# Conditioning weights stationary in TensorE in plain fp32, spread over three stages; layer 1's rows kept in SBUF; column block outermost in the dense matmuls

## The chip, the cores and the metric
The kernel runs on one core of a Trainium2 chip. The time is the device time of one execution in microseconds, as a median of several executions.

## The reference, cut to what matters
Two post-norm transformer layers over 1056 rows (1024 of a prompt, 32 of a sample) of width 1024, in fp32. Each layer first computes six conditioning vectors per sequence from a conditioning vector c, one c for the prompt and one for the sample:

```
mod = (silu(c) @ w_ada + b_ada)[:, None, :]        # w_ada: 1024 x 6144
sh1, sc1, g1, sh2, sc2, g2 = split(mod, 6)
u = layer_norm(x) * (1 + sc1) + sh1
... = split(u @ w_in)                              # queries, keys, values, gates
oa, ob, oc, state = mix_fn(...)                    # three groups of attention heads
o = concatenate([group_rms(oa), group_rms(ob), group_rms(oc)]) * g_out
x = layer_norm(ALPHA * x + g1 * (o @ w_out)) * ln1_g + ln1_b
u = layer_norm(x) * (1 + sc2) + sh2
f = square(relu(u @ w1)) @ w2                      # 1024 -> 4096 -> 1024
x = layer_norm(ALPHA * x + g2 * f) * ln2_g + ln2_b
```

The two columns of `silu(c)` are all that the conditioning multiplies: a matrix of 1024 x 6144 by two vectors. sh1 and sc1 are wanted first, g1 after the attention, sh2 and sc2 before the MLP, g2 in it. Outputs are the rows y and the attention caches.

## The kernel before, in words
A prologue and, per layer, a sequence of stages. Each stage is a block: all engines start it together and the next one starts when every queue is through. Inside a block each engine has its own queue in program order, and semaphores order the engines. SP issues all DMAs from its queue, in order.

- Prologue (L231 on): masks, silu(c) in `c_silu`, bias rows. SP copies the input rows into the output tensor `x_states`, and the block waits for that copy.
- Conditioning stage (L508 on): rows are loaded from `x_states` into `x_all` (nine tiles of 128 rows, the last of 32), VectorE takes mean and variance (`tile_stats`, `tile_figures`), POOL normalises the tiles in place (L539). The 24 chunks of w_ada (1 MB each, 128 x 2048, six buffers) are split by ScalarE and VectorE into two fp32r parts (L589, L617). TensorE holds `c_parts` as weights and streams the chunk in 16 pairs of 256 columns (L555): the result is a row of 256 values on 4 partitions, copied by ScalarE to `ada_v`. Once all chunks are through, small plain fp32 matmuls (L563: weights 4 x 128, 2 moving columns) turn the rows into columns: 16 of the 48 vectors' tiles before the first row tile is turned, then four after each further one. Then each row tile is turned by TensorE (`turn`, L445), scaled and shifted by ScalarE and VectorE (`scale_shift`, `scale_shift_rest`) and split into `u_hi` and `u_lo` (`split_turned`). POOL splits the first two weight chunks of the projection in the meantime (`pool_split`, L343, L345).
- Projection stage, attention stages: `three_pass` (L358) multiplies an fp32 weight chunk, split in two fp32r parts, with the split rows: three products of 128x128 weights with 352 columns, for each of three column blocks, each block in a PSUM bank of its own. The head outputs go to DRAM (`scr_o`).
- Output-projection stage (L1365 on): rows are loaded from `scr_o`, RMS-normalised (ScalarE L1411, VectorE L1448, POOL L1380), turned (L1391, L445), scaled by ScalarE (L1419), split by VectorE (L416, L418), and only when all nine tiles are through the projection begins (L1398).
- Post-norm stage (L1478 on): the projected columns are turned back (L1510) while SP loads the x tiles into two buffers (`x_tile`, L1485). VectorE adds and takes statistics (L1555). Two weight chunks for the MLP are loaded between x tile 3 and x tile 4 (L1493). Then the rows are normalised (ScalarE L1533), get gain (VectorE L1565) and bias (POOL L1501), are turned (L1517), copied to `acc` (ScalarE L1539, which takes its turn between the normalisations), normalised again (L1577), turned (L1522), modulated and split.
- MLP stage: 4608 matmuls of `three_pass`. Final stage (L1688 on): turned back, normalised, stored to `x_states[l + 1]`. After it POOL clears the layer's 148 semaphores one by one (L1756).

Of the kernel before, what the change touches and what calls it, by code (L numbers as in the profile page):

```python
# [17 lines left out]
F32 = mybir.dt.float32  # L18
# [42 lines left out]
def rows_of(t):  # L61
    return P if t < NPT else DEC

def build(nc, io):
    scr_o = nc.dram_tensor("scr_o", [T, D], F32, kind="Internal").ap()
    scr_a = nc.dram_tensor("scr_bias_a", [AH, P * EXT_A], F32, kind="Internal").ap()
# [16 lines left out]
    with ExitStack() as ctx:  # L84
# [17 lines left out]
        join = keep("join", [4, 2])  # L102
# [24 lines left out]
        ADA_SLOTS = 6  # L127
        ada_w = [at(f"w_ada{s}", U0 + s * 8192, [P, CW]) for s in range(ADA_SLOTS)]
        x_all = at("row_tiles", Q0 + 42240, [P, NTT, D])
        c_pad = at("c_zeros", U0 + ADA_SLOTS * 8192, [P, P])  # L130
        c_st = at("c_parts", U0 + ADA_SLOTS * 8192 + 512, [P, KT, P], F32R)
        ada_v = at("ada_rows", Q0 + 8192, [4, 256 * (ADA_CH + 2)])
# [96 lines left out]
        pro_ext, pro_edges, pro_x = sem("pro_ext_loaded"), sem("pro_ext_edges"), sem("pro_x_copied")  # L229
        with nc.Block() as block:  # L230
            @block.sync  # L231
            def _(sp):
# [8 lines left out]
                sp.dma_start(io["x_states"][0, 0:SEQ, :], io["x_prompt"][0]).then_inc(pro_x, 16)  # L241
                sp.dma_start(io["x_states"][0, SEQ:T, :], io["x_sample"][0]).then_inc(pro_x, 16)
# [6 lines left out]
                sp.wait_ge(pro_x, 64)  # L249
                sp.wait_ge(pro_bias, 16 * (1 + DEPTH))  # L250
# [23 lines left out]
            def _(dve):  # L274
# [16 lines left out]
                dve.tensor_tensor(join[:], ident[0:4, 0:2], ident[0:4, 2:4], ALU.add).then_inc(pro_act, 1)  # L291

# [4 lines left out]
        ada_in = [S(f"ada_loaded{s}") for s in range(ADA_SLOTS)]  # L297
        ada_hi, ada_lo, ada_used, par_in, mod_step, ada_sum, ada_clear, ada_turned, ada_c = S("ada_high"), S("ada_low"), S("ada_used"), S("params_loaded"), S("mod_steps"), S("ada_summed"), S("ada_margin"), S("ada_turned"), S("ada_c_parts")
# [59 lines left out]
        def three_pass(pe, out, s, cols, a_hi, a_lo):  # L358

            n = len(cols)
            for k, c in enumerate(cols):
                for w, a in ((w_hi, a_hi), (w_hi, a_lo), (w_lo, a_hi)):
                    for b in range(3):
                        mm = pe.matmul(out[:, b, :], w[s][:, c:c + P], a[:, k, b * NB:(b + 1) * NB],  # L365
                                       start=(k == 0 and w is w_hi and a is a_hi),
                                       stop=(k == n - 1 and w is w_lo))
            return mm
# [81 lines left out]
        row_in = [S(f"rows_loaded{t}") for t in range(NTT)]  # L450
# [55 lines left out]
        for l in range(DEPTH):  # L506

            with nc.Block() as block:  # L508
                @block.sync
                def _(sp):  # L510
                    for t in range(NTT):
                        r = rows_of(t)
                        sp.dma_start(x_all[0:r, t, :], io["x_states"][l, t * P:t * P + r, :]).then_inc(row_in[t], 16)
# [4 lines left out]
                    with sp.Fori(0, ADA_CH // ADA_SLOTS) as j:  # L518
                        for s in range(ADA_SLOTS):
                            sp.wait_ge(ada_lo, ADA_SLOTS * j + (s + 1))  # L520
                            sp.dma_start(ada_w[s][:], io["w_all"][l * CHUNKS + ADA_SLOTS * j + s]).then_inc(ada_in[s], 16)

# [3 lines left out]
                def _(pool):  # L526

                    own = Own(pool, ada_c)
                    own.did(pool.memset(c_pad[:], 0.0))
                    own.settle()  # L530
                    own.did(pool.tensor_copy(c_st[:, :, 4:P], c_pad[:, 4:P].rearrange("p (a b) -> p a b", a=1)
                                             .broadcast_to([P, KT, P - 4])))
                    own.did(pool.tensor_copy(c_st[:, :, 0:2], c_silu[:]))
                    own.settle()
                    own.did(pool.tensor_tensor(c_st[:, :, 2:4], c_silu[:], c_st[:, :, 0:2].bitcast(F32), ALU.subtract))
# [6 lines left out]
                    split_stream_free(pool)  # L542
                    pool.wait_ge(ada_used, ADA_CH + 2)
                    pool_weights(pool, 0, 2)

                @block.tensor
                def _(pe):
                    pe.sem_inc(ada_used, 2)
                    pe.wait_ge(ada_c, 4)
                    with pe.Fori(0, ADA_CH // ADA_SLOTS) as j:  # L550
                        for s in range(ADA_SLOTS):
                            pe.wait_ge(ada_lo, ADA_SLOTS * j + (s + 1 + ADA_SLOTS))
                            for k in range(KT):
                                for w in (w_hi, w_lo):
                                    mm = pe.matmul(psum[:, 4 + s % 2, 0:256], c_st[:, k, :],  # L555
                                                   w[s % 2][:, k * 256:(k + 1) * 256],
                                                   start=(k == 0 and w is w_hi), stop=(k == KT - 1 and w is w_lo))
                            mm.then_inc(ada_used, 1)

                    def turn_vectors(first, last):  # L560
                        for m in range(first, last):
                            c0 = 512 + m * P
                            mm = pe.matmul(psum[:, 6 + (first > 0), 2 * m:2 * m + 2], ada_v[:, c0:c0 + P], join[:],  # L563
                                           start=True, stop=True)
                        return mm
                    pe.wait_ge(ada_sum, ADA_CH + 2)
                    turn_vectors(0, 16).then_inc(ada_turned, 1)
# [7 lines left out]
                    mm.then_inc(ada_turned, 1)  # L575

                @block.scalar
                def _(act):
                    load_tables(act)
                    tile_roots(act, NTT, 1, r_var, r_log, r_root)  # L580
                    act.wait_ge(ada_clear, 1)
                    with act.Fori(0, ADA_CH // ADA_SLOTS) as j:
                        for s in range(ADA_SLOTS):
                            act.wait_ge(ada_in[s], 16 * j + 16)
                            act.wait_ge(ada_used, ADA_SLOTS * j + (s + 1))

                            act.activation(ada_v[:, bass.ds(256 * ADA_SLOTS * j + 256 * s, 256)],
                                           psum[0:4, 4 + s % 2, 0:256], ACT.Copy).then_inc(ada_sum, 1)
                            act.activation(w_hi[s % 2][:, 0:CW], ada_w[s][:], ACT.Copy).then_inc(ada_hi, 1)  # L589
                    for s in (ADA_SLOTS - 2, ADA_SLOTS - 1):  # L590
                        act.wait_ge(ada_used, ADA_CH + 2 - (ADA_SLOTS - 1 - s))
                        c0 = 256 * (ADA_CH + s - ADA_SLOTS + 2)
                        act.activation(ada_v[:, c0:c0 + 256], psum[0:4, 4 + s % 2, 0:256], ACT.Copy)\
                            .then_inc(ada_sum, 1)
                    for t in range(NTT):
                        if t == 0:
                            act.wait_ge(mod_step, 3)
# [4 lines left out]
                def _(dve):  # L602
                    own = Own(dve, a_dve)

                    dve.memset(psum[0:4, 4:6, 0:256], 0.0).then_inc(ada_clear, 1)
                    dve.sem_inc(ada_lo, ADA_SLOTS)
                    figures_begin(own)
                    for t in range(NTT):
                        dve.wait_ge(row_in[t], 16)
# [4 lines left out]
                    with dve.Fori(0, ADA_CH // ADA_SLOTS) as j:  # L614
                        for s in range(ADA_SLOTS):
                            dve.wait_ge(ada_hi, ADA_SLOTS * j + (s + 1))
                            dve.tensor_tensor(w_lo[s % 2][:, 0:CW], ada_w[s][:], w_hi[s % 2][:, 0:CW].bitcast(F32),  # L617
                                              ALU.subtract).then_inc(ada_lo, 1)

                    def vectors(n, first, last, scales):  # L620

                        dve.wait_ge(ada_turned, n + 1)
                        sums = psum[:, 6 + n, 0:96].rearrange("p (m c) -> p m c", c=2)
                        for c in range(2):
                            dve.tensor_tensor(mods[:, first:last, c], sums[:, first:last, c], b_ada[:, first:last],
                                              ALU.add).then_inc(mod_step, 1)
                        dve.wait_ge(mod_step, 3 * n + 2)
# [850 lines left out]
            with nc.Block() as block:  # L1478
                @block.sync
                def _(sp):  # L1480
# [366 lines left out]
```

## Time and profile before
| | us |
|---|---|
| median of 3 runs (3662.45 to 3667.59) | 3666.75 |
| the profiled execution, its own time | 3663.84 |
| span of its instructions | 3662.0 |

### The profile page before, as it was taken

The page shows a single profiled execution, that of the slowest core. Times are in us where ns is not written, and L with a number is a line of the kernel's source. Part 1 is how long each engine was busy: PE and PEld are TensorE (multiplying, and loading weights), DVE is VectorE, ACT ScalarE, POOL GpSimd, SP SyncE. Part 2 cuts the span into 40 slices and gives each one's busy share as a digit, 9 for nine tenths or more (in the row PEclk, how much of TensorE's full clock was granted, in tenths as well). Part 3 has the DMA queues.
Part 4 walks back from the last instruction along what each step waited for, and adds up shares of the span by engine and source line. Part 5 has one row for each costly group of instructions (what it writes and reads, how often), then busy time and mean ns, then how long its engine had stood idle before and what let it go on. Part 6 is the DMA issues. An engine that isn't in the chain of part 4 may idle for free. (4 is left out here: it accounts for less than half of the span.)

```text
span 3662.0 us, 50730 instructions
## 1 busy us (share of the span) xinstructions
PE 3098.5 (85%) x19938; PEld 2958.0 (81%) x19938; DVE 1521.5 (42%) x3371; ACT 917.2 (25%) x1906; POOL 1202.8 (33%) x567
## 2 busy tenths in 40 slices
PE   3799889669589999999537998896594899999994
PEld 3799879449489999999537997894493899999993
DVE  5501278450643333333655013884507333333335
ACT  3411266341320000000234113663413100000002
POOL 2122355111324444333221223651113333344441
PEclk9799999679689999999877998996795899999997
DMA  7322023320211111110173121233202111111101
GB/s 303 121 72 89 16 71 73 120 84 0 82 47 46 46 45 40 42 45 35 58 280 127 43 75 26 66 77 114 81 0 82 47 46 46 46 46 46 46 23 59
DMA packets 112569, 257.09 MB, mean 70 GB/s; under 512 B 42402, under 2 KB 78790, under 8 KB 94352
## 3 DMA queue, kind: packets, MB, share of 16 engines
q1 hardware_dynamic: 112416, 255.05, 20.5%
q8 instruction: 96, 1.57, 0.2%
q14 instruction: 57, 0.47, 0.0%
HBM read 216.40 MB, written 38.12 MB: 70 GB/s over the span
## 5 line engine op out<-in xcount | busy, mean ns | idle before, releaser
L343 POOL CAST w_hi<-w_raw 128x2048 fp32r<-128x2048 f32 (+1 forms) x92 | 174.4, 1896 | 1324.6 <-DVEq L1679 362.1
L365 PE MATMUL psum<-u_hi,w_hi 128*128 128x352 f32 x2592 | 565.5, 327 | 19.6 <-ACT L209 9.2
L365 PE MATMUL psum<-u_lo,w_hi 128*128 128x352 f32 x2592 | 562.7, 326 | 0.0
L365 PE MATMUL psum<-u_hi,w_lo 128*128 128x352 f32 x2592 | 561.6, 325 | 0.0
L1682 DVE SCALAR_TENSOR_TENSOR acc_t<-psum,mods,acc_t 128x704 f32<-128x704 f32 (+2 forms) x768 | 401.0, 578 | 298.6 <-PE psum L365 298.6
L365 PEld LDWEIGHTS psum<-u_hi,w_hi 128*128 128x128 f32 x2592 | 445.8, 190 | 20.8 <-issue 20.7
L345 POOL TENSOR_TENSOR w_lo<-w_raw,w_hi 128x2048 fp32r<-128x2048 f32 (+1 forms) x92 | 450.5, 4897 | 7.4
L365 PEld LDWEIGHTS psum<-u_lo,w_hi 128*128 128x128 f32 x2592 | 447.2, 190 | 0.0
L365 PEld LDWEIGHTS psum<-u_hi,w_lo 128*128 128x128 f32 x2592 | 443.5, 190 | 0.0
L1669 DVE TENSOR_TENSOR h_relu<-h_relu 128x1056 f32<-128x1056 f32 x64 | 103.1, 1612 | 696.6 <-ACT h_relu L1659 696.6
L1659 ACT ACTIVATE h_relu<-psum 128x1056 f32<-128x1056 f32 x64 | 67.5, 1054 | 1161.8 <-PE psum L365 1161.8
L365 PE MATMUL psum<-h_hi,w_hi 128*128 128x352 f32 x1536 | 332.3, 324 | 0.0
L365 PE MATMUL psum<-h_lo,w_hi 128*128 128x352 f32 x1536 | 329.8, 323 | 0.0
L365 PE MATMUL psum<-h_hi,w_lo 128*128 128x352 f32 x1536 | 329.0, 323 | 0.0
L1612 POOL TENSOR_TENSOR h_lo<-h_relu,h_hi 128x1056 fp32r<-128x1056 f32 x64 | 158.2, 2472 | 379.6 <-ACT h_hi L1661 370.0
L445 PE MATMUL psum<-ident,row_tiles 128*128 128x128 f32 (+1 forms) x576 | 130.3, 406 | 159.5 <-POOL row_tiles L1501 48.3
L365 PEld LDWEIGHTS psum<-h_hi,w_hi 128*128 128x128 f32 x1536 | 263.3, 188 | 0.0
L365 PEld LDWEIGHTS psum<-h_lo,w_hi 128*128 128x128 f32 x1536 | 260.8, 188 | 0.0
L365 PEld LDWEIGHTS psum<-h_hi,w_lo 128*128 128x128 f32 x1536 | 259.7, 188 | 0.0
L445 PEld LDWEIGHTS psum<-ident,row_tiles 128*128 128x128 f32 (+1 forms) x576 | 106.9, 220 | 178.5 <-POOL row_tiles L1501 55.5
L555 PE MATMUL psum<-w_hi,c_parts 128*128 128x256 f32 x384 | 108.0, 315 | 165.6 <-DVE w_lo L617 165.0
L555 PEld LDWEIGHTS psum<-w_hi,c_parts 128*128 128x128 f32 x384 | 81.0, 211 | 175.2 <-DVE w_lo L617 175.2
(198 smaller groups left out, 5091.5 us busy)
## 6 DMA issues: line engine op xcount, KB each, us to landing
w_raw<-in_w_all SPq DMA_DIRECT2D x86, 1024.0 KB, 4.8
w_ada<-in_w_all SPq DMA_DIRECT2D x48, 1024.0 KB, 5.6
row_tiles<-out_x_states SPq DMA_DIRECT2D x16, 512.0 KB, 7.2
scr_o<-o_head SPq DMA_DIRECT2D x32, 256.0 KB, 2.7
row_tiles<-scr_o SPq DMA_DIRECT2D x16, 512.0 KB, 7.1
x_tile<-out_x_states SPq DMA_DIRECT2D x16, 512.0 KB, 4.3
out_x_states<-row_tiles SPq DMA_DIRECT2D x16, 512.0 KB, 2.7
w_raw<-in_w_v SPq DMA_DIRECT2D x6, 1032.0 KB, 4.8
```

The costliest lines, as they stand in the source:

```text
L343: pool.tensor_copy(w_hi[s][:, 0:c], raw[s][:, 0:c]).then_inc(pool_step, 1)
L345: pool.tensor_tensor(w_lo[s][:, 0:c], raw[s][:, 0:c], w_hi[s][:, 0:c].bitcast(F32), ALU.subtract).then_inc(pool_step, 1)
L365: mm = pe.matmul(out[:, b, :], w[s][:, c:c + P], a[:, k, b * NB:(b + 1) * NB], start=(k == 0 and w is w_hi and a is a_hi), stop=(k == n - ...
L445: mm = pe.transpose(dst[:, k, 0:r], src[0:r, k * P:(k + 1) * P], ident[0:r, 0:r])
L555: mm = pe.matmul(psum[:, 4 + s % 2, 0:256], c_st[:, k, :], w[s % 2][:, k * 256:(k + 1) * 256], start=(k == 0 and w is w_hi), stop=(k == KT ...
L1612: pool.tensor_tensor(h_lo[par][:, m, :], h_r[m][:], h_hi[par][:, m, :].bitcast(F32), ALU.subtract).then_inc(h_rdy, 1)
L1659: act.activation(h_r[m][:].rearrange("p (b c) -> p b c", c=NB), lin[m], ACT.Relu).then_inc(h_ev[m], 1)
L1669: dve.tensor_tensor(h_r[m][:], h_r[m][:], h_r[m][:], ALU.mult).then_inc(h_sqd, 1)
L1682: ins = dve.scalar_tensor_tensor(a, lin[m % 2][:, b0:b1, c0:c1], mods[:, 40 + m, c:c + 1], a, ALU.mult, ALU.add)
```

## The change
The chunks of w_ada are no longer split. Each of their 128x128 blocks stands in TensorE as weights, in plain fp32, and the two columns of `c_silu` are the moving operand, so that the result comes out as columns in one PSUM bank and nothing has to be turned. Of the 24 chunks eight stay in the conditioning stage, eight go between the turns of the output-projection stage, eight between the two groups of turns of the post-norm stage; `add_bias` adds b_ada where each eight are through. The rows of layer 0 and its first eight chunks are loaded in the prologue; in layer 1 the rows are those that the final stage left in `x_all`, and its first eight chunks are loaded during that stage. `x_states` is gone: x tiles are read from the inputs or from a DRAM tensor between the layers. `three_pass` now goes through the column blocks outermost and takes (w_hi, a_hi), (w_lo, a_hi), (w_hi, a_lo) in each. The post-norm stage uses two PSUM tiles in turn instead of four.

```diff
+        def conditions(pe, chunk, w):
+            for m in (2 * chunk, 2 * chunk + 1):
+                for k in range(KT):
+                    c0 = 256 * k + P * (m % 2)
+                    mm = pe.matmul(psum[:, 6, 2 * m:2 * m + 2], w[:, c0:c0 + P], c_silu[:, k, :],
+                                   start=(k == 0), stop=(k == KT - 1))
+            return mm
+        def add_bias(dve, first, last, scales, done):
+            sums = psum[:, 6, 0:96].rearrange("p (m c) -> p m c", c=2)
+            for c in range(2):
+                dve.tensor_tensor(mods[:, first:last, c], sums[:, first:last, c], b_ada[:, first:last],
+                                  ALU.add).then_inc(mod_step, 1)
...
@@ three_pass
-            for k, c in enumerate(cols):
-                for w, a in ((w_hi, a_hi), (w_hi, a_lo), (w_lo, a_hi)):
-                    for b in range(3):
+            for b in range(3):
+                for k, c in enumerate(cols):
+                    for w, a in ((w_hi, a_hi), (w_lo, a_hi), (w_hi, a_lo)):
...
@@ prologue, SP
-                sp.dma_start(io["x_states"][0, 0:SEQ, :], io["x_prompt"][0]).then_inc(pro_x, 16)
-                sp.dma_start(io["x_states"][0, SEQ:T, :], io["x_sample"][0]).then_inc(pro_x, 16)
+                for t in range(NTT):
+                    sp.dma_start(x_all[0:rows_of(t), t, :], x_rows(0, t)).then_inc(row_x[t], 16)
+                    if t < 8:
+                        sp.dma_start(ada_w[t][:], io["w_all"][t]).then_inc(ada_in[t], 16)
...
@@ conditioning stage, TensorE (the splits on ScalarE and VectorE, and turn_vectors, are gone)
+                    for s in range(8):
+                        pe.wait_ge(ada_in[s], 32 * l + 16)
+                        conditions(pe, s, ada_w[s]).then_inc(ada_mm, 1)
                     for t in range(NTT):
                         pe.wait_ge(a_xn, t + 1)
...
                         turn(pe, tr2[t % 2], x_all[:, t, :], rows_of(t), a_turned)
-                        if 1 <= t <= 8:
-                            mm = turn_vectors(12 + 4 * t, 16 + 4 * t)
...
@@ output-projection stage, SP and TensorE
+                    for n, c in enumerate(ADA_F):
+                        if n >= 4:
+                            sp.wait_ge(ada_mm, 8 + n - 3)
+                        sp.dma_start(ada_f[n % 4][:], io["w_all"][l * CHUNKS + c]).then_inc(ada_fin[n % 4], 16)
                     sp_weights(sp, l, IN_CH + 2, OUT_CH - 2)
...
                         turn(pe, tr2[t % 2], x_all[:, t, :], rows_of(t), f_turned)
+                        if t >= 1:
+                            pe.wait_ge(ada_fin[(t - 1) % 4], 16 * ((t - 1) // 4 + 1))
+                            conditions(pe, ADA_F[t - 1], ada_f[(t - 1) % 4]).then_inc(ada_mm, 1)
...
@@ post-norm stage, SP and TensorE
                     for t in range(2, NTT):
                         x_tile(t)
                         if t == 3:
+                            for s, c in enumerate(ADA_G):
+                                sp.dma_start(ada_w[s][:], io["w_all"][l * CHUNKS + c]).then_inc(ada_in[s], 16)
                             sp_weights(sp, l, UP0, 2)
...
                         mm.then_inc(g_back, 1)
+                    for s, c in enumerate(ADA_G):
+                        pe.wait_ge(ada_in[s], 32 * l + 32)
+                        conditions(pe, c, ada_w[s]).then_inc(ada_mm, 1)
                     for t in range(NTT):
                         pe.wait_ge(g_x1, t + 1)
...
@@ final stage, SP
+                    if l + 1 < DEPTH:
+                        for s in range(8):
+                            sp.dma_start(ada_w[s][:], io["w_all"][(l + 1) * CHUNKS + s]).then_inc(ada_in[s], 16)
```

## Rows read from the trace of the kernel before
**Rows 1.** The page, parts 1 and 2: span, TensorE's busy time, its clock.
```profile
span 3662.0 us, 50730 instructions
...
PE 3098.5 (85%) x19938; PEld 2958.0 (81%) x19938; DVE 1521.5 (42%) x3371; ACT 917.2 (25%) x1906; POOL 1202.8 (33%) x567
...
PEclk9799999679689999999877998996795899999997
```
**Rows 2.** Busy time by stretch: from:to, length, engines, clock, DMA share, GB/s.
```profile
19.73:172.70 152.97, 92.82 (x552) 86.20 (x552) 97.97 (x101) 73.67 (x108) 33.34 (x17) 0.84 0.53 207
782.30:831.50 49.20, 15.80 (x72) 12.90 (x72) 34.10 (x79) 26.07 (x93) 13.52 (x9) 0.53 0.35 131
928.90:1034.50 105.60, 47.27 (x216) 37.89 (x217) 83.66 (x130) 41.46 (x78) 34.82 (x13) 0.56 0.20 72
1034.50:1781.30 746.80, 744.83 (x4608) 744.54 (x4608) 250.93 (x416) 68.53 (x64) 287.72 (x92) 1.00 0.12 42
1843.70:1993.90 150.20, 88.16 (x552) 81.39 (x552) 100.76 (x101) 73.60 (x107) 35.63 (x17) 0.77 0.55 211
```
**Rows 3.** Timeline of TensorE, layer 1's conditioning: start, duration, line, count, idle before.
```profile
1952.51 3.73 PE L563 MATMUL psum<-join,ada_rows 4*128 4x2 f32 x32 [0.46 <-ACT ada_rows L593]
1956.16 3.59 PE L445 MATMUL psum<-ident,row_tiles 128*128 128x128 f32 x16
1959.68 1.05 PE L563 MATMUL psum<-join,ada_rows 4*128 4x2 f32 x8
```
**Rows 4.** L563 by stretch: PE busy (x), PEld busy (x), clock, DMA share, GB/s.
```profile
1952.50:1956.10 3.60, 3.60 (x32) 3.60 (x32) 1.00 0.00 0
1956.20:1959.60 3.40, 0.03 (x1) 0.00 (x0) 0.51 0.00 0
147.90:149.80 1.90, 1.86 (x8) 1.78 (x8) 0.50 0.00 0
```
**Rows 5.** SP's issues from 0 to 180 us; GB/s in 40 slices of 20:60.
```profile
19.74 4.97 SPq L513 DMA_DIRECT2D row_tiles<-out_x_states  x9
...
GB/s 61 324 414 311 266 340 369 401 418 422 426 418 173 16 174 426 410 418 442 442 401 426 451 426 401 418 442 418 410 410 451 426 410 418 336 410 393 344 393 328
```
**Rows 6.** Timeline of POOL and VectorE, layer 0's conditioning stage.
```profile
39.89 19.78 POOL L539 TENSOR_SCALAR row_tiles<-row_tiles,tile_rsqrt 128x1024 f32<-128x1024 f32 x9 [18.44 <-DVE tile_rsqrt L408]
130.78 1.89 POOL L343 CAST w_hi<-w_raw 128x2048 fp32r<-128x2048 f32 x1 [71.11 <-PE psum L555]
132.76 4.51 POOL L345 TENSOR_TENSOR w_lo<-w_raw,w_hi 128x2048 fp32r<-128x2048 f32 x1
...
140.16 4.50 DVE L416 CAST u_hi<-turned_tile 128x1024 fp32r<-128x1024 f32 x1 [0.67 <-ACT turned_tile L428]
```
**Rows 7.** Timeline of TensorE, the front of layer 0's output projection.
```profile
801.98 3.68 PE L445 MATMUL psum<-ident,row_tiles 128*128 128x128 f32 x16 [22.44 <-POOL row_tiles L1380]
815.07 1.97 PE L445 MATMUL psum<-ident,row_tiles 128*128 128x128 f32 x8 [1.37 <-DVE u_lo L418]
821.35 1.97 PE L445 MATMUL psum<-ident,row_tiles 128*128 128x128 f32 x8 [1.37 <-DVE u_lo L418]
```
**Rows 8.** Timeline of POOL between the layers.
```profile
1843.76 0.20 POOL L529 MEMSET c_zeros<- 128x128 f32 x1 [13.76 <-POOLq L1757]
```
**Rows 9.** Layer 0's post-norm stage: timeline of TensorE, and a wait of VectorE.
```profile
949.16 1.97 PE L1510 MATMUL psum<-ident,attn_t 128*128 128x128 f32 x8 [2.84 <-DVE row_tiles L1555]
968.96 1.97 PE L445 MATMUL psum<-ident,row_tiles 128*128 128x128 f32 x8 [12.59 <-POOL row_tiles L1501]
...
DVE row_tiles L1555 <- DMA x_tile<-out_x_states: 7.9, 3, 3.1
```
**Rows 10.** Pitch: seven steps of the old conditioning (timeline); the value projection by stretch.
```profile
1948.74 0.28 PE L555 MATMUL psum<-w_hi,c_parts 128*128 128x256 f32 x1
1949.56 0.28 PE L555 MATMUL psum<-w_lo,c_parts 128*128 128x256 f32 x1
...
245.00:328.00 83.00, 81.58 (x648) 77.47 (x648) 1.00 0.21 76
```

More of the change, by code:

```diff
@@ L66, in build, with x_rows @@
     scr_o = nc.dram_tensor("scr_o", [T, D], F32, kind="Internal").ap()
+    x_mid = nc.dram_tensor("x_between_layers", [T, D], F32, kind="Internal").ap()
+    def x_rows(l, t):
+        if l == 0:
+            return io["x_prompt"][0, t * P:(t + 1) * P, :] if t < NPT else io["x_sample"][0]
+        return (x_mid if l == 1 else io["y_rows"])[t * P:t * P + rows_of(t), :]
     scr_a = nc.dram_tensor("scr_bias_a", [AH, P * EXT_A], F32, kind="Internal").ap()
@@ L228, in build @@
             sem("pro_loaded"), sem("pro_steps"), sem("pro_exp"), sem("pro_matmul"), sem("pro_bias_stored"))
-        pro_ext, pro_edges, pro_x = sem("pro_ext_loaded"), sem("pro_ext_edges"), sem("pro_x_copied")
+        pro_ext, pro_edges, pro_x = sem("pro_ext_loaded"), sem("pro_ext_edges"), sem("pro_selectors_loaded")
+        row_x = [sem(f"x_rows_loaded{t}") for t in range(NTT)]
+        ada_in = [sem(f"ada_loaded{s}") for s in range(8)]
         with nc.Block() as block:
@@ L296, in build @@
         pool_turn = S("pool_chunks_begun")
-        ada_in = [S(f"ada_loaded{s}") for s in range(ADA_SLOTS)]
-        ada_hi, ada_lo, ada_used, par_in, mod_step, ada_sum, ada_clear, ada_turned, ada_c = S("ada_high"), S("ada_low"), S("ada_used"), S("params_loaded"), S("mod_steps"), S("ada_summed"), S("ada_margin"), S("ada_turned"), S("ada_c_parts")
+        ada_fin = [S(f"ada_f_loaded{s}") for s in range(4)]
+        par_in, mod_step, ada_mm = S("params_loaded"), S("mod_steps"), S("ada_done")
+        def conditions(pe, chunk, w):
[10 more added lines that the diff above has]
+                                  ALU.add).then_inc(mod_step, 1)
+            if scales is not None:
+                dve.wait_ge(mod_step, done - 1)
+                dve.tensor_scalar(mods[:, scales:scales + 8, :], mods[:, scales:scales + 8, :], 1.0, None, ALU.add)\
+                    .then_inc(mod_step, 1)
         def split_stream_free(eng):
@@ L517, in _ @@
                     sp.dma_start(b_f[:], io["b_f"][bass.ds(l, 1), :].broadcast_to([P, CH])).then_inc(par_in, 16)
[L518 to L521, printed above, removed]
+                    if l == 0:
+                        sp.wait_ge(pro_bias, 16 * (1 + DEPTH))
+                        sp.wait_ge(pro_x, 32)
                     sp_weights(sp, l, 0, 2)
@@ L526, in _ @@
                 def _(pool):
[L528 to L535, printed above, removed]
+                    split_stream_free(pool)
                     pool.wait_ge(a_shift, 1)
@@ L547, in _ @@
                 def _(pe):
[L548 to L567, printed above, removed]
+                    for s in range(8):
+                        pe.wait_ge(ada_in[s], 32 * l + 16)
+                        conditions(pe, s, ada_w[s]).then_inc(ada_mm, 1)
                     for t in range(NTT):
@@ L580, in _ @@
                     tile_roots(act, NTT, 1, r_var, r_log, r_root)
[L581 to L594, printed above, removed]
+                    act.wait_ge(mod_step, 3)
                     for t in range(NTT):
-                        if t == 0:
-                            act.wait_ge(mod_step, 3)
                         act.wait_ge(a_turned, t + 1)
@@ L613, in _ @@
                     tile_figures(own, LN_EPS, 1, r_var, r_root, a_shift)
[L614 to L627, printed above, removed]
-                        dve.tensor_scalar(mods[:, scales:scales + 8, :], mods[:, scales:scales + 8, :], 1.0, None, ALU.add)\
-                            .then_inc(mod_step, 1)
                     dve.wait_ge(par_in, 64)
-                    vectors(0, 0, 16, 8)
+                    dve.wait_ge(ada_mm, 8)
+                    add_bias(dve, 0, 16, 8, 3)
                     for t in range(NTT):
@@ L634, in _ @@
                         split_turned(own, t, a_hi, a_lo)
-                    vectors(1, 16, 48, 32)
             K_EV = K_TILES
@@ L1516, in _ @@
                             pe.wait_ge(g_acc, t - 1)
-                        turn(pe, tr2[1 + t % 2], x_all[:, t, :], rows_of(t), g_x1t)
+                        turn(pe, tr2[t % 2], x_all[:, t, :], rows_of(t), g_x1t)
+                    pe.wait_ge(g_acc, NTT)
                     for t in range(NTT):
@@ L1521, in _ @@
                             pe.wait_ge(g_lo, t - 1)
[L1522 removed]
+                        turn(pe, tr2[t % 2], x_all[:, t, :], rows_of(t), g_xnt)
                 @block.scalar
@@ L1554, in _ @@
                         dve.wait_ge(g_back, t + 1)
-                        own.did(dve.scalar_tensor_tensor(y, x_sl[s][0:r, :], ALPHA, wide[3 * s][0:r, :],
+                        own.did(dve.scalar_tensor_tensor(y, x_sl[s][0:r, :], ALPHA, wide[s][0:r, :],
                                                          ALU.mult, ALU.add), g_y)
```

54 lines of the change are left out of this document (22 added, 32 removed).

## Prediction
> **What bounds the kernel now.** I read the page first, then the span cut at the stage borders, then the timelines of the stages that the diff touches. TensorE is busy 85% of the span [rows 1], and the cut says where not [rows 2]. The MLP (1034.5 to 1781.3) is TensorE at full clock without a gap: nothing there can be won but the pitch of its matmuls. The stages that the change edits are the other kind. The conditioning stage takes 153 us in layer 0 and 150 us in layer 1, the output-projection front (rows normalised and turned) 49 us with TensorE busy 15.8, the post-norm stage 105.6 us with TensorE busy 47.3, at a mean granted clock of 0.53 and 0.56. They are chains through four engines in which TensorE's queue waits. So each part is priced as a delay of such a chain.
>
> **What one chunk of conditioning costs after the change.** `conditions` issues 2 x 8 plain fp32 matmuls per chunk, 128x128 weights against 2 moving columns. The nearest operation of the trace is the turning of the vectors at L563: 128-column fp32 weights, 2 moving columns, plain fp32. It leaves two records per matmul (96 matmuls, 192 records). At full clock 32 records take 3.60 us (0.112 each); at half clock 8 take 1.86 us, which is seven steps of 0.213 and the last one's own length [rows 3, 4]. A chunk is 16 matmuls, 32 records: 3.6 us at full clock, 32 x 0.213 = 6.8 us at half. Eight chunks are 28.7 or 54.6 us; a layer has three such eights, 164 us of TensorE at half clock against 24 x 3.43 us = 82 now.
>
> **Which clock.** This decides the sign, and the trace has one passage on it. In layer 1 TensorE ran 1952.51 to 1956.24 nothing but L563 records, back to back, at granted clock 0.99; in the stretch right behind them the mean is 0.51, though transposes follow without a gap [rows 3, 4]. After the same number of transposes on end, 1956.16 to 1959.75, the next eight L563 records take 1.05 us, full clock again. In the interleaved part (a turn, eight L563 records, a turn) it stays at half [rows 3]. So a stream of two-column matmuls did not hold the full clock. I take half clock, 6.8 us per chunk. Against it: L563's weights fill 4 partitions, the new ones 128, and no row shows a long stream of those with few moving columns.
> The Trainium skill (TensorE: Matmul & The Clock Gate, "Why this matters for your kernels") says to keep TensorE continuously busy to get to the full clock. By that rule the conditioning streams run at 2.4 GHz and the change comes out faster; the L563 rows speak against it. It is the first rival below.
>
> **Layer 0, conditioning stage.** Now: a block switch at 19.7 behind the copy of the input rows, 24 chunks until 131, turns from 135.85, dense work from 172.88. After: the copy is gone and the prologue's SP issues 17 loads instead, 17 x 0.55 us (nine take 4.97 [rows 5]) from 3.64, then its three small stores: the stage starts at about 14.5. The loads are 12.6 MB; the queues moved about 0.42 MB per us [rows 5], so they land until about 36. VectorE's statistics end with the last row tile, thus POOL's normalising starts at about 39.2 against 39.89 now, and ends at 59; its two weight splits (12.9 us [rows 6]) end at 72. TensorE starts chunk 0 at 14.5 and is never short of data: 14.5 + 54.6 = 69. Then the turns. What follows was 37 us (135.85 to 172.88). The L563 records between the turns go; next late is the chain of turn, ScalarE, VectorE's cast and subtraction, two tiles deep: the output-projection front has exactly it, 6.28 us per two tiles (815.07 to 821.35) [rows 7]. First split at 74 (VectorE's cast took 4.50 us beside POOL's split [rows 6], which ends at 72), 7 x 3.15 more, last tile and block switch 2.5: dense work at 99. **Saved: 74.**
> **Layer 1.** The rows stay in SBUF and the eight chunks are loaded during the layer before, so TensorE starts at once: 1842.5 + 54.6 = 1897; statistics 14.7 (nine tiles of 1.63), POOL's 21.5 and 12.9 end at 1893 beside it. Then 6.4 for the first tile, 22 for seven, 2.5: dense work at 1928 against 1994.1. **Saved: 66**, of which 1.2 because 17 fewer of the 148 semaphores are cleared between the layers (POOL stands idle 13.76 us there, at most 0.09 us each [rows 8]). The same clearing at the end of the program: **1.2.**
>
> **Output-projection front, both layers.** Chunk t-1 stands in TensorE's queue behind turn t. Behind it wait the next turn, ScalarE, VectorE's split and then the projection. Now TensorE works from 801.98 to the border at 831.5, at the chain's pace [rows 2, 7]. After: eight turns of 1.71, the short one 0.9, eight chunks of 6.8: 69.2 us, TensorE bound, dense work at 871.5. The chunks' loads (behind the row loads on the queue) land by 799 to 807; a chunk reloaded after release has 30 us. The two weight loads now behind them on SP have 50 us. ScalarE's wait for the vectors is long met at its first read. **Lost: 40 per layer** (9 at full clock: 9 x 4.6 from 801.98).
>
> **Post-norm stage, both layers.** Two things add up. First the queue: SP issues eight 1 MB chunks between x tile 3 and x tile 4. Already two 1 MB weight loads there make tile 4 late: turn 5's successor starts after a 2.84 us wait for VectorE, which waited for x tiles 7.9 us in three times [rows 9]. Eight more MB at 0.42 MB per us are 19 to 20 us in front of tile 4; VectorE's row sums wait, and with them the turns back. Then, in order in TensorE's queue, all eight chunks stand ahead of the first turn of the new rows. Now TensorE idles 12.59 us there. After: turns back end at 956.4 (968.96 less the idle 12.59) + 19 = 975.4, chunks 54.6 to 1030, first turn 1030 instead of 968.96. The three tiles ready by then shorten the following by 0.7, the bias adds on VectorE cost 0.5; ScalarE cannot run ahead, as its copies wait for these very turns. A window of full clock now and then takes back 1. **Lost: 60 per layer.** Using two PSUM tiles instead of four adds a wait for the ninth copy, which is over (997.3) before the norm (1000.0).
>
> **Order of the dense matmuls.** 12,384 matmuls of 352 columns, each with its own weight load before and after. Pitch now 744.83 / 4608 = 161.6 ns, 0.459 ns per column, the PSUM bank changing each time. The old conditioning kept one bank and changed the weights each time: 0.82 us for seven steps of 256 columns, 117 ns, 0.458 per column [rows 10]. Same per column, so I take 0. Bounds: below, 352 columns at 2.4 GHz, 146.7 ns, or -185 us; above, the value projection (L741, one bank, 258 columns), 81.58 / 648 = 126 ns with its handovers, 0.488 per column, +126 us. I go by the old conditioning's rows: only they are free of handovers.
>
> **Sum.** -74 - 66 - 1.2 + 2 x 40 + 2 x 60 = +59 us. The profiled execution took 3663.84 us around its span of 3662.0; the median of the runs is 2.9 us above. 3666.75 + 59 = about 3725 us.
>
> **Rivals.**
> First, TensorE holds the full clock in the conditioning streams (weights of 128 partitions being the difference). A chunk is then 3.6 us. Layer 0: mods at 45, the rest bound by POOL's rows and its splits' hold on VectorE, dense at 78, saved 95; layer 1: dense at 1908, saved 86; lost 9 in each front and 19 + 28.7 + 3 - 12.6 - 1 = 37 in each post-norm stage. Sum -95 - 86 - 1 + 92 = -90: 3577 us, faster. For it: the transposes on end in rows 3 brought the clock back at once. It decides from where chunks average under about 5.6 us: six groups of eight chunks are 48 chunk times on the path, and 59 / 48 = 1.2 us less per chunk brings the sum to nothing. Chance 0.28.
> Second, the new matmul order changes the pitch: 5 ns less, an estimate of a third of the way from 161.6 to 146.7, gives -62 with the half clock: 3664, no change; 5 ns more gives 3787. For it: nothing in rows 10; against: equal cost per column in both patterns. Chance 0.06 down, 0.03 up.
> Third, the clock is mixed: full where turns stand between the chunks (the fronts), half in the streams: +59 - 62 = -3, 3664. Against it: the interleaved L563 and turns ran at half [rows 3]. Chance 0.06.
> That the loads in the post-norm stage do not hold the x tiles back changes little: TensorE's 54.6 us then start 19 earlier, 2 x 19 less, 3687; inside the forecast's case.
>
> **How the numbers follow.** Half clock as forecast 0.57; its own range is 3690 to 3755 (from the last remark to ten more microseconds in each of the four delays with some lost saving). With the first rival (3577, give or take 20) at 0.28, the range that leaves out no more than 2 in 10 runs from 3560 to 3755. Within 0.2% (7 us, what a measurement of this kernel can tell from no change) comes 0.05 of the 0.12 around 3664 (second rival downward, third rival); of the rest 0.04 lie below and 0.03 above. Faster: 0.28 + 0.04 = 0.32. Slower: 0.57 + 0.03 + 0.03 = 0.63.
>
> **What would show it.** The granted clock in the first 50 us of the stage that holds `conditions`, and the time of 32 of its records: 6.8 or 3.6 us. Dense work of layer 0 at about 99 (78 if full), the fronts 89 us long instead of 49, the post-norm stages 166 instead of 106, x tile 4 landing some 20 us later after its issue. The MLP at 746.8 us shows the order neutral; 10 us either way says not. The prediction is wrong if a chunk takes under 5 us, or if the MLP moves by more than 10.

## The result, and the profile after

| kernel | median of its runs, us (lowest to highest) | ratio to the kernel before (95% interval) | profiled execution: time, span, mean granted clock |
|---|---|---|---|
| before | 3664.6 (3655.4 to 3667.6) | | 3663.84, 3662.0, 0.903 |
| after | 3724.9 (3711.5 to 3734.5) | 1.0153 (1.0126 to 1.0179) | 3711.45, 3709.4, 0.880 |

The change makes the kernel 1.5% slower: 60 us by the medians, 47.6 us between the two profiled executions, which are what the stages below are read from. The forecast was 3725.

The page of the kernel after: span, busy time by engine, TensorE's granted clock in 40 slices (before: [rows 1]).
```profile
span 3709.4 us, 51265 instructions
PE 3252.7 (88%) x20514; PEld 3128.8 (84%) x20514; DVE 1394.0 (38%) x3324; ACT 812.0 (22%) x1806; POOL 1180.9 (32%) x559
PEclk9999997768579999999859999967775899999997
```
TensorE is busier (3252.7 against 3098.5 us) and the kernel slower: the new work is matmuls at half clock. Where it stands is seen by stage. The same view as [rows 2], for the kernel after: layer 0's conditioning stream, the front of its output projection, its post-norm stage, its MLP, and the conditioning stage of layer 1.
```profile
21.00:75.80 54.80, 54.73 (x257) 54.77 (x258) 14.37 (x34) 1.70 (x3) 23.53 (x13) 1.00 0.39 152
713.80:798.90 85.10, 65.47 (x328) 65.40 (x329) 33.93 (x79) 26.12 (x93) 13.45 (x9) 0.52 0.46 175
895.10:1059.60 164.50, 101.30 (x472) 93.13 (x472) 83.24 (x133) 41.29 (x78) 34.84 (x13) 0.53 0.25 97
1059.60:1801.80 742.20, 740.18 (x4608) 739.92 (x4608) 250.93 (x416) 68.56 (x64) 287.81 (x92) 1.00 0.12 43
1862.40:1946.50 84.10, 70.91 (x328) 68.21 (x328) 36.80 (x73) 20.96 (x58) 23.54 (x13) 0.50 0.07 26
```
The first row's clock of 1.00 is no measurement: the trace has no entry of the granted clock before 78.5 us, and the mean of 0.880 counts that time as full clock too. The durations tell it there: 256 records in 54.6 us are 0.213 each, the same as in the post-norm stage, where the entry is there and reads 0.50. These are the records of `conditions` alone (L310): the eight chunks of layer 0's first stage, the eight of its post-norm stage, and the first two chunks of its front.
```profile
21.00:75.60 54.60, 54.53 (x256) 54.57 (x256) 1.00 0.39 152
940.80:995.20 54.40, 54.40 (x256) 54.40 (x256) 0.50 0.00 1
736.90:740.60 3.70, 3.70 (x32) 3.70 (x32) 0.95 0.01 2
742.20:748.90 6.70, 6.67 (x32) 6.70 (x32) 0.50 0.35 142
```
So a chunk takes 6.8 us (54.6 / 8), as forecast. One ran almost wholly at full clock (0.95), right behind 16 transposes on end; then the clock fell and stayed down.

The stages one by one, each from its table load to the next one's. The two profiled executions differ by 47.4 us of span, and the stages add up to it:

| part | forecast | measured |
|---|---|---|
| dense work of layer 0 begins | -74 | -67.6 (172.9 to 105.3) |
| layer 1: conditioning stage and the clearing before it | -66 | -67.9 (150.2 to 84.1; 62.4 to 60.6) |
| clearing at the end | -1.2 | -1.3 |
| two fronts of the output projection | +80 | +73.4 (34.7 and 38.7) |
| two post-norm stages | +120 | +120.3 (104.2 to 163.1; 103.2 to 164.6) |
| two MLPs | 0 | -10.0 (748.3 to 743.6; 748.8 to 743.5) |
| QKV projection, attention, sample attention | 0 | +0.5 |
| sum | +59 | +47.4 |

The front. Timeline of TensorE in the kernel after (start, duration, line, operation, count, idle before), as [rows 7]:
```profile
733.43 3.67 PE L470 MATMUL psum<-ident,row_tiles 128*128 128x128 f32 x16 [22.38 <-POOL row_tiles L1339]
736.89 3.82 PE L310 MATMUL psum<-c_silu,w_ada_f 128*128 128x2 f32 x32
740.58 1.85 PE L470 MATMUL psum<-ident,row_tiles 128*128 128x128 f32 x8
742.23 6.83 PE L310 MATMUL psum<-c_silu,w_ada_f 128*128 128x2 f32 x32
...
792.11 6.99 PE L310 MATMUL psum<-c_silu,w_ada_f 128*128 128x2 f32 x32
798.95 0.64 PE L390 MATMUL psum<-u_hi,w_hi 128*128 128x352 f32 x1
```
No wait stands between 736.89 and the first matmul of the projection at 798.95: the engine that used to wait for the chain is now what the chain waits for.

The post-norm stage. TensorE first, then SP's queue (the second number is the time that the issues take on SP) and VectorE's waits for the x tiles (in all, times, longest), against [rows 9]:
```profile
908.45 1.97 PE L1478 MATMUL psum<-ident,attn_t 128*128 128x128 f32 x8 [0.69 <-DVE row_tiles L1528]
933.78 1.97 PE L1478 MATMUL psum<-ident,attn_t 128*128 128x128 f32 x8 [23.37 <-DVE row_tiles L1528]
...
939.10 1.89 PE L1478 MATMUL psum<-ident,attn_t 128*32 128x128 f32 x8 [0.69 <-DVE row_tiles L1528]
940.78 54.61 PE L310 MATMUL psum<-c_silu,w_ada 128*128 128x2 f32 x256
995.25 5.18 PE L470 MATMUL psum<-ident,row_tiles 128*128 128x128 f32 x24
1003.14 1.64 PE L470 MATMUL psum<-ident,row_tiles 128*128 128x128 f32 x8 [2.70 <-POOL row_tiles L1469]
```
```profile
903.17 4.29 SPq L1460 DMA_DIRECT2D w_ada<-in_w_all  x8
907.50 0.95 SPq L356 DMA_DIRECT2D w_raw<-in_w_all  x2
908.50 28.24 SPq L1451 DMA_DIRECT2D x_tile<-in_x_prompt  x4
...
DVE row_tiles L1528 <- DMA x_tile<-in_x_prompt: 26.4, 3, 22.6
```
Both delays of the forecast stand there. The wait that was 2.84 us is 23.37: eight 1 MB chunks and two weight loads were issued ahead of x tile 4, which was issued at 908.50 and landed at 932.49 (before: 941.67 and 947.86), and VectorE waited 22.6 us for it at a stretch. And where TensorE had idled 12.59 us ahead of the new rows' first turn, it now works through 54.61 us of chunks first; at 995.25 three tiles are ready.

The start. SP's issues in the prologue of the kernel after (beginnings of the stretches, and what they take):
```profile
3.62 0.43 SPq L249 DMA_DIRECT2D row_tiles<-in_x_prompt  x1
...
9.37 0.49 SPq L251 DMA_DIRECT2D w_ada<-in_w_all  x1
9.90 1.93 SPq L249 DMA_DIRECT2D row_tiles<-in_x_prompt  x1
11.87 1.80 SPq L251 DMA_DIRECT2D w_ada<-in_w_all  x1
...
16.80 2.68 SPq L249 DMA_DIRECT2D row_tiles<-in_x_sample  x1
19.53 0.32 SPq L254 DMA_DIRECT2D bias_a_rows<-ext_a_row  x1
```
Twelve of the 17 loads take half a microsecond each, the last five 1.5 to 2.7: the stage begins at 21.0 and not at 14.5. Behind it, POOL's normalising and its second weight split, and VectorE's first cast:
```profile
40.94 11.54 POOL L550 TENSOR_SCALAR row_tiles<-row_tiles,tile_rsqrt 128x1024 f32<-128x1024 f32 x9 [39.03 <-DVE tile_rsqrt L433]
61.49 4.51 POOL L370 TENSOR_TENSOR w_lo<-w_raw,w_hi 128x2048 fp32r<-128x2048 f32 x1
79.96 0.69 DVE L441 CAST u_hi<-turned_tile 128x1024 fp32r<-128x1024 f32 x1 [0.67 <-ACT turned_tile L453]
```
POOL is through at 66.0, ten microseconds before the last chunk (75.6), and the cast takes 0.69 us and not 4.50.

### The profile page after: what moved, and what is told of

Read it like the earlier page. It is cut to its first block and busy times, and to the rows that moved or that the text cites. A ratio compares the mean times of both kernels' runs of the same rounds, so it can differ in the third digit from the quotient of the medians.

```text
span 3709.4 us, 51265 instructions
## 1 busy us (share of the span) xinstructions
PE 3252.7 (88%) x20514; PEld 3128.8 (84%) x20514; DVE 1394.0 (38%) x3324; ACT 812.0 (22%) x1806; POOL 1180.9 (32%) x559
## 5 line engine op out<-in xcount | busy, mean ns | idle before, releaser
L390 PE MATMUL psum<-u_hi,w_hi 128*128 128x352 f32 x2592 | 842.0, 325 | 16.4 <-ACT L214 9.2
L390 PE MATMUL psum<-u_lo,w_hi 128*128 128x352 f32 x2592 | 842.2, 325 | 0.0
L390 PE MATMUL psum<-u_hi,w_lo 128*128 128x352 f32 x2592 | 841.5, 325 | 0.0
L390 PEld LDWEIGHTS psum<-u_hi,w_hi 128*128 128x128 f32 x2592 | 492.1, 190 | 17.4 <-issue 17.3
L390 PE MATMUL psum<-h_hi,w_lo 128*128 128x352 f32 x1536 | 495.3, 322 | 0.0
L390 PE MATMUL psum<-h_lo,w_hi 128*128 128x352 f32 x1536 | 495.0, 322 | 0.0
L390 PE MATMUL psum<-h_hi,w_hi 128*128 128x352 f32 x1536 | 494.3, 322 | 0.0
L390 PEld LDWEIGHTS psum<-u_hi,w_lo 128*128 128x128 f32 x2592 | 491.5, 190 | 0.0
L310 PE MATMUL psum<-c_silu,w_ada 128*128 128x2 f32 x1024 | 218.7, 352 | 59.9 <-PEq L1735 43.8
L310 PEld LDWEIGHTS psum<-c_silu,w_ada 128*128 128x128 f32 x1024 | 218.8, 333 | 61.6 <-issue 61.5
```

The source lines that it names most:

```text
L310: mm = pe.matmul(psum[:, 6, 2 * m:2 * m + 2], w[:, c0:c0 + P], c_silu[:, k, :], start=(k == 0), stop=(k == KT - 1))
```

## The experiments

**The clock.** One theory: the chunks run at half clock because their matmuls move only two columns. The rival: the matmuls' kind (plain fp32, a new 128x128 weight block for each) keeps the clock down whatever they move. The vector is moved 64 times over, so that 128 columns pass; the sums fall on columns that a later matmul overwrites or nobody reads, and the instructions are as many as before.
```diff
-  mm = pe.matmul(psum[:, 6, 2 * m:2 * m + 2], w[:, c0:c0 + P], c_silu[:, k, :],
+  mm = pe.matmul(psum[:, 6, 2 * m:2 * m + P].rearrange("p (a b) -> p a b", b=2), w[:, c0:c0 + P],
+                 c_silu[:, k:k + 1, :].broadcast_to([P, P // 2, 2]),
```

> The changed kernel with the moving operand of the conditioning matmuls widened from 2 to 128 columns: the same two columns repeated 64 times by a stride of zero, 126 result columns unused. Theory (half clock is due to the narrow moving operand, and the 128-column fp32 weight load hides 128 moving columns): 32 records of a chunk take 6.8 us at half clock as before, the clock rises to full, and then 3.6 us; conditioning stages fall by some 20 us (bound by POOL and the turns there), fronts by 25 to 30, post-norm stages by 24: 3725 to about 3575. Rival A (the clock stays at half whatever the width, since plain fp32 does not raise it): no change, 3725. Rival B (moving columns add to the weight load): a chunk takes 13.7 us at half clock and 7.2 at full, 3725 or up to 4050.

Measured: 3571.9 us (3561.8 to 3577.3), ratio 0.9736 (0.9715 to 0.9757). TensorE in the front and in the post-norm stage, then layer 0's front, its post-norm stage and layer 1's conditioning stage by stretch, and last the records of `conditions` alone (L310) in the post-norm stage:
```profile
722.66 4.03 PE L310 MATMUL psum<-c_silu,w_ada_f 128*128 128x128 f32 x32
726.52 1.04 PE L471 MATMUL psum<-ident,row_tiles 128*128 128x128 f32 x8
727.39 3.74 PE L310 MATMUL psum<-c_silu,w_ada_f 128*128 128x128 f32 x32
...
898.22 29.96 PE L310 MATMUL psum<-c_silu,w_ada 128*128 128x128 f32 x256
```
```profile
699.80:757.40 57.60, 38.21 (x327) 38.05 (x328) 34.17 (x79) 26.13 (x93) 13.53 (x9) 0.80 0.68 258
852.00:991.50 139.50, 76.68 (x472) 68.00 (x473) 83.24 (x133) 41.28 (x78) 34.85 (x13) 0.63 0.29 115
1794.30:1860.70 66.40, 45.20 (x328) 42.65 (x328) 44.20 (x73) 21.10 (x58) 24.07 (x13) 0.73 0.09 33
...
898.30:900.60 2.30, 2.30 (x12) 2.30 (x13) 0.50 0.03 7
900.70:928.00 27.30, 27.30 (x246) 27.29 (x244) 1.00 0.00 1
```
Sixty-four times the columns, and 256 records take 29.96 instead of 54.61 us. At full clock the records of a chunk follow each other every 0.112 us, with two columns (the chunk at 736.89, once the clock is up) as with 128, so there the columns cost nothing that can be seen; at half clock it is 0.213 with two and 0.222 with 128. And the same stream of weights, without a gap, stays at 1.2 GHz with two moving columns, and with 128 goes to 2.4 GHz within its first chunk and stays there. No run tries a width in between, so how few columns would do is open. The whole time comes out near where the forecast's first rival had put full clock (3577).

**The two parts of the post-norm delay, and the front.** Loads moved behind the x tiles:
```diff
     for t in range(2, NTT):
         x_tile(t)
         if t == 3:
-            for s, c in enumerate(ADA_G):
-                sp.dma_start(ada_w[s][:], io["w_all"][l * CHUNKS + c]).then_inc(ada_in[s], 16)
             sp_weights(sp, l, UP0, 2)
+    for s, c in enumerate(ADA_G):
+        sp.dma_start(ada_w[s][:], io["w_all"][l * CHUNKS + c]).then_inc(ada_in[s], 16)
```

> The changed kernel; in the post-norm stage SP issues the eight chunk loads after the last x tile instead of after x tile 3. Theory (the queue holds x tile 4 back and TensorE's chunks then start 19 to 20 us later): the wait of 23.37 us in the turns back goes, the turns back end some 20 us earlier, chunks follow at once, each layer's post-norm stage falls from 163 to about 144 us: 3725 to about 3686. Rival (the row sums' delay is hidden, since TensorE's chunks are the bound either way and would only wait for their own loads): the stage stays within 5 us, 3715 to 3725.

Measured: 3688.6 us (3680.9 to 3691.1), ratio 1.0058 (1.0038 to 1.0077); the stages take 146.8 and 148.1 us instead of 163.1 and 164.6. TensorE there:
```profile
921.55 1.97 PE L1478 MATMUL psum<-ident,attn_t 128*128 128x128 f32 x8 [3.33 <-DVE row_tiles L1528]
...
932.13 54.77 PE L310 MATMUL psum<-c_silu,w_ada 128*128 128x2 f32 x256 [3.39 <-DMA w_ada<-in_w_all]
```
The wait of 23.37 is 3.33 (it was 2.84 before the change). The stage gains 16.3 and 16.5 us, 3.6 less than the 20.0 of that wait, mostly because chunk 0 now waits 3.39 us for its own load. The time also agrees with the 3687 that the forecast's last remark on the rivals gives for this case.

The chunks' matmuls taken out, once in the front and once in the post-norm stage, their loads kept:
```diff
-  conditions(pe, ...).then_inc(ada_mm, 1)
+  pe.sem_inc(ada_mm, 1)
```

> The changed kernel without the conditioning matmuls of the output-projection front; its eight 1 MB loads per layer stay, the gate vectors g1 and the first MLP vectors are not computed. Theory (TensorE's 54.6 us per layer in that queue are the whole cost): the fronts fall back by what they grew, 35 to 39 us per layer: 3725 to about 3650. Rival (the loads on SP's queue delay rows or weights there): part of the growth stays, the time is over 3670.

> The changed kernel without the conditioning matmuls of the post-norm stage; its eight 1 MB loads between x tile 3 and x tile 4 stay, the second shift, scale and gate vectors are not computed. Theory (two terms in one chain: the queue's 20 us, then TensorE's 54.6 less the 12.6 it idled): the wait of some 23 us before the turn back after x tile 4 stays, the stage goes from 163 to about 122 us, not to the 104 of before, so 3725 - 2 x 41 = about 3643. Rival (the whole growth is TensorE's): the stage goes to 104 us, 3607.

Measured without the front's: 3637.1 us (3634.5 to 3648.4), ratio 0.9933 (0.9912 to 0.9954). The output projections with their fronts take 146.3 and 145.9 us, as before the change (146.6, 146.5): the whole loss there, 35 and 39 us, is these matmuls, and nothing of it the loads. (The median lies 13 us under the 3650 expected; between the profiled executions the fall is 77.0 us, of which these two stages are 74.3.) Measured without the post-norm's: 3646.6 us (3633.7 to 3647.4), ratio 0.9943 (0.9927 to 0.9958), stages 123.0 and 124.3 us. TensorE in it:
```profile
947.48 1.97 PE L1478 MATMUL psum<-ident,attn_t 128*128 128x128 f32 x8 [23.44 <-DVE row_tiles L1528]
...
967.27 1.11 PE L470 MATMUL psum<-ident,row_tiles 128*128 128x128 f32 x4 [12.59 <-POOL row_tiles L1469]
```
Here the queue's delay is left alone (23.44), and the old idle time of 12.59 is back. The stage's 60 us are thus 19 to 21 us of queue (123.0 - 104.2, 124.3 - 103.2) and 40 of TensorE (163.1 - 123.0, 164.6 - 124.3), near the 42 that 54.6 less the idle 12.6 gives.

**The start.** Four chunks' loads instead of eight in the prologue, the other four in the first stage:
```diff
-   if t < 8:
+   if t < 4:
        sp.dma_start(ada_w[t][:], io["w_all"][t]).then_inc(ada_in[t], 16)
...
    if l == 0:
+       for s in range(4, 8):
+           sp.dma_start(ada_w[s][:], io["w_all"][s]).then_inc(ada_in[s], 16)
```

> The changed kernel with four of the eight chunk loads of layer 0 moved from the prologue to the head of the conditioning stage. In the changed kernel SP's issues stall from the fifteenth load on (1.5 to 2.7 us each) and the stage starts at 21.0 instead of 14.5. Theory: with four loads fewer the prologue ends at about 12 to 14, TensorE starts its chunks 6 to 8 us earlier, and with a bound of 54.6 us of TensorE the layer's dense work comes as much earlier: 3725 to about 3718. Rival (the start is set by the last landing): no change.

Measured: 3713.7 us (3710.9 to 3723.2), ratio 1.0142 (1.0126 to 1.0157). TensorE at the block switch:
```profile
13.04 54.74 PE L310 MATMUL psum<-c_silu,w_ada 128*128 128x2 f32 x256 [8.07 <-PEq L237]
```
The stage begins 8 us earlier and is as long as before (84.1), so 8 us are won in the profile. The stall sets in with the thirteenth load, not the fifteenth as the expectation has it, and here too the thirteenth, now the last, is the first slow one (1.88 us, 128 KB). In the ratios the intervals of the two kernels overlap; the stage shows it, the whole time only leans that way.

**The order of the dense matmuls.** The whole order of the change on the kernel before; then its block loop alone; then its order of products alone (there the block loop stays innermost).
```diff
-  for k, c in enumerate(cols):
-      for w, a in ((w_hi, a_hi), (w_hi, a_lo), (w_lo, a_hi)):
-          for b in range(3):
+  for b in range(3):
+      for k, c in enumerate(cols):
+          for w, a in ((w_hi, a_hi), (w_lo, a_hi), (w_hi, a_lo)):
...
```

> The kernel before with the new order of three_pass alone (column block outermost, w_hi and w_lo on the same moving columns in succession). If the order is what made the MLP stage 4.7 and 5.3 us shorter in the changed kernel (pitch 160.6 instead of 161.6 ns), the two MLP stages fall from 748.5 to about 743.5 us each here too, and the whole by 10 to 12 us (3664 to about 3653, ratio 0.997). If the shorter MLP came from something else in the change, pitch stays at 161.6 and the time at 3664.

> The kernel before with the column block outermost but the products in the old order, (w_hi, a_hi), (w_hi, a_lo), (w_lo, a_hi). If the 1 ns of pitch comes from staying in one PSUM bank, the MLP stages are 743.5 us as with the whole new order; if it comes from the two products in succession on the same moving columns, they stay at 748.5.

> The kernel before with the products in the order (w_hi, a_hi), (w_lo, a_hi), (w_hi, a_lo) but the column block still innermost. The block order alone gave MLP stages of 745.7 and 745.4 us, pitch 161.0, half of the way from 748.5 to 743.3. If each of the two edits gives its half, the stages are about 746 here too; if the product order works only where the same moving columns come in direct succession, which needs the block outermost, they stay at 748.5.

Measured: the whole order 3661.4 us (3644.5 to 3671.6), ratio 0.9986 (0.9971 to 1.0002), so the 10 to 12 us expected are not shown by the whole time. The block loop alone 3661.9 and the products alone 3674.9 us, one execution each, from which no difference of whole times can be read: the sample attention, which neither touches, took 118.6 us in each layer of the second and in layer 0 of the first, against 106.2 to 115.7 elsewhere. The MLP's stretch can be read: the 16 MLP stages of the eight profiled kernels with the whole new order took 742.5 to 743.8 us, the two before the change 748.3 and 748.8, with the block loop alone 745.7 and 745.4, with the products alone 743.7 and 744.6. Layer 0 in these three kernels, in this order:
```profile
1028.60:1768.30 739.70, 739.60 (x4608) 739.34 (x4608) 249.42 (x413) 68.53 (x64) 287.86 (x92) 1.00 0.12 43
```
```profile
1037.40:1779.80 742.40, 742.30 (x4608) 742.04 (x4608) 249.37 (x413) 68.66 (x64) 287.91 (x92) 1.00 0.12 43
```
```profile
1042.60:1783.00 740.40, 740.31 (x4608) 740.05 (x4608) 249.44 (x413) 68.64 (x64) 287.83 (x92) 1.00 0.12 43
```
TensorE's busy time divided by 4608: 160.50, 161.09 and 160.66 ns, against 161.64 before [rows 2] and 160.63 after. The order of products alone gives 0.98 of the 1.14 ns (4.6 and 4.2 us of the stages' 5.3 and 5.1), although the bank still changes with each matmul; the block loop alone gives 0.55; the two do not add. So the expectation's second case, that the order of products does nothing while the block loop stays innermost, is wrong. Why it saves something stays open: in that kernel neither the moving columns nor the bank stay the same from one matmul to the next, and the weights change more often than before (after three matmuls, where it was after six and three), so reuse of any of them does not explain it. For the kernel it is 5 us per MLP, under what whole times can tell.

**All of it together:** 128 moving columns, late loads, four chunks in the prologue, on the kernel after.

> The three repairs together: 128 moving columns, chunk loads of the post-norm stage behind the x tiles, four chunk loads moved out of the prologue. From 3572 of the wide one: 2 x 18 less in the post-norm stages and 0 to 6 less at the start: about 3532. If the queue term is hidden once the chunks are short, 3570.

Measured: 3531.5 us (3524.1 to 3547.8), ratio 0.9652 (0.9629 to 0.9675), the fastest of the kernels here. Its conditioning stage, front and post-norm stage in layer 0:
```profile
13.10:82.40 69.30, 45.30 (x328) 42.57 (x328) 44.24 (x73) 20.97 (x58) 24.04 (x13) 0.77 0.41 168
694.50:753.80 59.30, 39.22 (x329) 39.06 (x330) 33.90 (x79) 26.03 (x93) 13.44 (x9) 0.80 0.67 251
848.30:971.00 122.70, 76.12 (x472) 67.17 (x472) 83.27 (x133) 41.23 (x78) 34.83 (x13) 0.66 0.33 130
```
By the stage borders the conditioning stage is 69.2 us, where the kernel before has 153.0; the front with its projection 153.8, where it has 146.6; the post-norm stage 121.4, where it has 104.2. Eight chunks are some 30 us of TensorE, yet they cost the front 7.2 us and the post-norm stage 17.2, since they partly fill time in which TensorE had waited.

## Why the prediction was right

**The price of a chunk, and the clock.** Right: 6.8 us, from the L563 rows [rows 3, 4]. Weights on 128 partitions, the argument left for the rival, did not bring the full clock with two moving columns; the moving-column run shows that their number is the reason. The rule of the Trainium skill (TensorE: Matmul & The Clock Gate, "Why this matters for your kernels") that keeping TensorE continuously busy gets it to full clock does not hold for this stream: 54.6 us back to back in four places, at half clock throughout (in three by the clock's entries, in the first by the durations). Once its condition was met, the rival's 3577 was right to 5 us (3571.9), but by errors that cancel: between the profiled executions the start saves 83 us and not 95, the fronts lose 12 in all and not 18, the MLPs give 10, and the projection and attention stages happen to be 11 longer, 8.7 of it in layer 1's sample attention.

**Layer 0, start.** The step that failed: "17 loads instead, 17 x 0.55 us" for SP's issues. Beyond the twelfth each took 1.5 to 2.7 us, so the stage began at 21.0 and not 14.5, and 67.6 us were saved instead of 74. The run with four chunks fewer in the prologue shows that the loads are the cause: it starts at 13.0. From the start on the forecast held: 84.3 us to the dense work (105.3 - 21.0), forecast 84.5. In that, one step did not happen: the forecast had POOL at its splits until 72 and the first cast slowed to 4.50 us beside them. POOL's normalising took 11.54 us where it had taken 19.78 [rows 6], POOL was through at 66.0, before the chunks, and the cast took 0.69 us; the chunks alone set the time, 29.7 us from their end to the dense work against the forecast's 30. The misjudged step cost the forecast little, since its chain for layer 1, without POOL in it, comes to 30.9 us (6.4 + 22 + 2.5). With short chunks the forecast's hold is there: in the 128-column run POOL splits until 67.0, and the first two casts take 2.83 and 4.18 us.

**Layer 1.** Right: 66.1 us of the stage and 1.8 of the clearing, forecast 66 in all.

**Fronts.** Right in mechanism, shown by leaving the matmuls out. The size was 40 each and came to 34.7 and 38.7; in layer 0 one chunk at full clock (3.82) makes 3 us of the difference. The price at full clock, 9, does not follow from its working (9 x 4.6 from 801.98 ends 12 us behind 831.5); with 128 columns the stages grew by 5.8 and 6.0.

**Post-norm stages.** Right in both parts: queue 19 and TensorE 54.6 less the idle 12.59 were the main terms, 60 the sum; measured 58.9 and 61.4, parted by two runs into about 20 and 40.

**Order of the matmuls.** "Same per column, so I take 0" was wrong in size and not in what it means for the answer: -4.7 and -5.3 us in the two MLPs, inside the 10 that the forecast allowed and the -185 to +126 of its bounds. The rows of the old conditioning that I went by [rows 10] keep the bank and load weights for each matmul, though by L555 of the kernel before the same ones twice in succession and not new ones each time; they hold one order of products only, and a row of 0.82 us given to 0.01 cannot show a difference of 0.6%.

**The sum.** +47.4 in the span against +59: the start brought 6.4 less than forecast, the fronts lost 6.6 less, the MLPs gave 10, layer 1 1.9 more. The medians say +60, which agrees with 3725 better than the steps deserve: that last agreement is luck. Times of one kernel scatter by 5 to 27 us, and the untouched sample attention alone took between 106.2 and 118.6 us in different executions.

## What to carry to other kernels

A matrix-vector product that is moved to TensorE by making the weights stationary is priced here in weight blocks, not in columns; look for rows of few-column matmuls and their clock, and where they run at half, try a wider moving operand, which here cost nothing at full clock and turned a loss of 1.5% into a gain of 2.6%. Work that is "spread" over later stages is free only where its engine's queue and the DMA queue in front of it both had room: here 8 MB ahead of a needed tile cost 16 to 21 us, and the chunks ahead of the turns their whole length less the 12.6 us in which TensorE had idled. Adding up the delays at the stage borders, with the idle time that each swallows, gave every stage to within 6.5 us.

## What the runs showed of the hardware

- With 128x128 fp32 weights and two moving columns TensorE's granted clock stays at 0.50 (1.2 GHz) over 54.6 us without a gap; with 128 moving columns and everything else equal it rises within the first chunk (in the post-norm stage after 2.4 us) and stays at 1.00 to the end of the 29.96 us.
- A plain fp32 matmul with new 128x128 weights takes two records, 0.112 us from one to the next at full clock with two moving columns as with 128, and 0.213 (two) or 0.222 (128) at half.
- DMA issues on SP took 0.5 us for the first twelve loads of 0.5 to 1 MB in a row, then 1.5 to 2.7 us each; with 13 loads in the prologue only the last was slow.
- With ten 1 MB loads ahead of it in SP's queue a 0.5 MB tile landed 24.0 us after its issue, with two 6.2 us.
- The order in which three products are summed changed the pitch of 352-column matmuls from 161.6 to 160.7 ns, with weights, columns and banks as many and as large as before (one profiled execution of that kernel, two MLP stages); the cause is open.
